# Attention heads in pairs, the recurrent part's preparation moved ahead of the second attention, and small matmuls in idle stretches of a two-block transformer kernel

## What is computed

```
state = state * wt + sa * bt + vt * kt        # per head, 64 x 64, sa = state @ at
y = state @ rt
```

## Time and profile before

| | |
|---|---|
| runs | 2500.05, 2499.9, 2498.51 us, median 2499.9 |
| profiled execution | 2497.89 us, its span 2496.2 us |
| mean granted clock of PE | 0.941 |
| bytes read | 614.26 MB, 246 GB/s over the span |
| instructions | 35200 |

### The profile page before, as it was taken

The page is one execution under the profiler, slowest core; times in us unless marked ns, Lnnn a source line. Parts: engine busy times, 40 slices in busy tenths (PEclk is TensorE's granted clock), DMA queues, the critical chain, the costliest instruction groups (busy, mean ns, idle before and its releaser), DMA issues.

```text
span 2496.2 us, 35200 instructions
## 1 busy us (share of the span) xinstructions
PE 2269.5 (91%) x14178; PEld 1936.6 (78%) x14178; DVE 1726.6 (69%) x1706; ACT 1370.3 (55%) x1273; POOL 93.4 (4%) x154
## 2 busy tenths in 40 slices
PE   4997999799799999999999999987995886999986
PEld 2966899795788888888888888876975785888876
DVE  1764444635578888888888888855446447899954
ACT  2225333435367777777777777753443234677743
POOL 8300000001000000000000000000000000000000
PEclk7998999899799999999999999998987887999988
DMA  8665765348259999999999999977620131899930
GB/s 261 198 204 175 238 233 187 113 152 281 91 203 368 379 372 370 371 371 371 370 373 370 370 371 367 375 226 101 192 64 2 36 135 46 306 371 374 371 137 18
DMA packets 339250, 618.72 MB, mean 248 GB/s; under 512 B 24609, under 2 KB 165154, under 8 KB 339087
## 3 DMA queue, kind: packets, MB, share of 16 engines
q1 hardware_dynamic: 339086, 616.43, 70.7%
HBM read 614.26 MB, written 1.05 MB: 246 GB/s over the span
## 4 chain that ended last, share of the span: by engine, by line
PE 88%; DVE 6%; ACT 2%; issue 2%; SPq 1%; DMA 1%; DVEq 0%; POOL 0%; ACTq 0%; POOLq 0%
PE bank L1146 11%; PE bank L1147 11%; PE bank L1148 11%; PE bank L2045 6%; PE bank L2046 6%; PE bank L2047 6%; PE bank L1178 5%; PE bank L1180 5%; PE bank L1176 5%; PE bank L2082 2%; PE bank L2155 2%; PE bank L2116 1%; PE bank L1119 1%; PE bank L2111 1%; PE bank L1156 1%
## 5 line engine op out<-in xcount | busy, mean ns | idle before, releaser
L1351 DVE TENSOR_TENSOR ring_lo<-ring_raw,ring_hi 128x2048 fp32r<-128x2048 f32 x432 | 988.1, 2291 | 140.1 <-ACT ring_hi L1261 139.5
L1261 ACT ACTIVATE ring_hi<-ring_raw 128x2048 fp32r<-128x2048 f32 x432 | 827.8, 1920 | 289.2 <-PE bank L1148 181.4
L1146 PE MATMUL bank<-ring_hi,xg_hi 128*128 128x512 f32 x1152 | 458.0, 398 | 2.1 <-DVE xg_lo L1451 2.1
L1147 PE MATMUL bank<-ring_hi,xg_lo 128*128 128x512 f32 x1152 | 451.0, 391 | 0.0
L1148 PE MATMUL bank<-ring_lo,xg_hi 128*128 128x512 f32 x1152 | 450.7, 391 | 0.0
L2045 PE MATMUL bank<-Hh,ring_hi 128*128 128x256 f32 x1048 | 307.2, 293 | 56.3 <-DVE ring_lo L454 23.0
L454 DVE TENSOR_TENSOR ring_lo<-ring_raw,ring_hi 128x2048 fp32r<-128x2048 f32 (+1 forms) x96 | 218.0, 2282 | 188.3 <-ACT ring_hi L436 165.1
L2046 PE MATMUL bank<-Hl,ring_hi 128*128 128x256 f32 x1048 | 303.9, 290 | 0.0
L2047 PE MATMUL bank<-Hh,ring_lo 128*128 128x256 f32 x1048 | 303.6, 290 | 0.0
L2045 PEld LDWEIGHTS bank<-Hh,ring_hi 128*128 128x128 f32 x1048 | 209.0, 199 | 59.6 <-issue 48.5
L1146 PEld LDWEIGHTS bank<-ring_hi,xg_hi 128*128 128x128 f32 x1152 | 217.5, 189 | 48.0 <-ACT xg_hi L1304 2.9
(11 more groups left out here) (475 smaller groups left out, 2764.3 us busy)
## 6 DMA issues: line engine op xcount, KB each, us to landing
ring_raw<-in_moe_w SPq DMA_DIRECT2D x672, 512.0 KB, 5.2
ring_raw<-in_ada_w SPq DMA_DIRECT2D x96, 512.0 KB, 5.9
ring_raw<-in_ffn_w SPq DMA_DIRECT2D x66, 512.0 KB, 4.9
ring_raw<-in_exp_gate SPq DMA_DIRECT2D x64, 512.0 KB, 4.8
ring_raw<-in_exp_up SPq DMA_DIRECT2D x64, 512.0 KB, 4.7
ring_raw<-in_exp_down SPq DMA_DIRECT2D x64, 512.0 KB, 4.7
ring_raw<-in_w_in SPq DMA_DIRECT2D x42, 512.0 KB, 4.9
ring_raw<-in_conv_in_w SPq DMA_DIRECT2D x16, 512.0 KB, 8.4
```

The costliest lines, as they stand in the source:

```text
L1146: mm(o, xg_hi[:, g, kk, :], wh(k), start=(kk == 0), stop=False)
L1147: mm(o, xg_lo[:, g, kk, :], wh(k), start=False, stop=False)
L1261: run(ring_hi[:, s, :], ring_raw[:, n % RAW, :], ACT.Copy).then_inc(T.sem("hi_done"), 1)
L1351: tt(ring_lo[:, s, :], ring_raw[:, n % RAW, :], ring_hi[:, s, :].bitcast(F32), ALU.subtract).then_inc(T.sem("lo_done"), 1)
```

## The change

1. **Preparation.** Its steps are cut into functions and put between the column units of block 2, on PE, ACT and DVE. Its tiles get other homes, for the old ones are in use then. The head mask `m_d64` is built on POOL after "shifted", not after a2. ACT waits for "decayed" ahead of a2's softmax.
2. **Heads in pairs.** `attention` goes over pairs: the scores of two heads are issued alternately into two banks, their values alternately into two halves of one bank. The rings `pr` and `small` have four slots, not three, and ACT evicts outputs later.
3. **Convolution.** Block 5 keeps 17 of its 31 taps on PE; DVE adds the other 14 after PE's sum is evicted. PE has 79 taps, five between two adaptive units.
4. **Splits.** At the feed-forward's end the last split ahead of ln1 is the one two units ahead, not three.
5. **Small matmuls.** `keep_busy(n)` issues n fp32 matmuls of 128 columns, whose results nobody reads, into the bank that is next to be taken: six between mean and variance of all nine layer norms, and 16 to 28 at other places, 302 in all.
6. **Tokens of the second expert stage** are written contiguously, and PE reads its stationary blocks with a step of four elements.

The diff, cut to its core (the moved functions `lora_pe`, `gate_lora_pe`, `head_sums_pe`, `shift_act`, `lora_act`, `gate_lora_act`, `norm_act`, `decay_act`, `keys_dve`, `decay_dve`, `norm2_dve`, `mixed_key_dve`, `normal_dve`, `bonus_dve` and `decayed_dve` hold the same operations as before, in part on other tiles, and are left out; `normal_dve` does them in two halves):

```diff
+            pairs = heads // 2
+            half = lambda h: (h // 2, slice(64 * (h % 2), 64 * (h % 2) + 64))
+
+            def scores(j):
+                b = [take(pe, f"{name} s {2 * j + n}") for n in range(2)]
+                pe.eng.wait_ge(*T.at(f"{name} qT {j // 2}"))
+                pe.eng.wait_ge(*T.at(f"{name} kT {j // 2}"))
+                for n in range(2):
+                    k, r = half(2 * j + n)
+                    mm(b[n][:, 0:P], Q[r, k, 0:P], K[r, k, 0:P], start=True, stop=True)
+                for n in range(2):
+                    k, r = half(2 * j + n)
+                    mm(b[n][:, P:3 * P], Q[r, k, P:S], K[r, k, :], start=True, stop=True)\
+                        .then_inc(pe.tick(f"mm {name} s {2 * j + n}"), 1)
+
+            def turned(j):
+                for h in (2 * j, 2 * j + 1):
                     b = take(pe, f"{name} pT {h}", "B")
                     pe.eng.wait_ge(*T.at(f"{name} p {h}"))
                     for c in range(3):
-                        last = nc.tensor.transpose(b[:, c * P:(c + 1) * P], pr[:, h % 3, c * P:(c + 1) * P],
+                        last = nc.tensor.transpose(b[:, c * P:(c + 1) * P], pr[:, h % 4, c * P:(c + 1) * P],
                                                    ident[:, :])
                     last.then_inc(pe.tick(f"mm {name} pT {h}"), 1)
-                if i >= 3:
-                    h = i - 3
-                    k, r = h // 2, slice(64 * (h % 2), 64 * (h % 2) + 64)
-                    if h % 2 == 0:
-                        bank_o[k] = take(pe, f"{name} o {k}", "C")
-                    b = bank_o[k]
-                    pe.eng.wait_ge(*T.at(f"{name} pT {h}"))
-                    pe.eng.wait_ge(*T.at(f"{name} v"))
-                    hs = slice(64 * h, 64 * h + 64)
-
-                    mm(b[r, 0:S], V[:, 0, hs], prT[:, h % 3, 0:2 * P], start=True, stop=False,
+
+            def values(j):
+                b = take(pe, f"{name} o {j}", "C")
+                pe.eng.wait_ge(*T.at(f"{name} v"))
+                for n in range(2):
+                    pe.eng.wait_ge(*T.at(f"{name} pT {2 * j + n}"))
+                for n in range(2):
+                    h = 2 * j + n
+                    mm(b[half(h)[1], 0:S], V[:, 0, 64 * h:64 * h + 64], prT[:, h % 3, 0:2 * P], start=True, stop=False,
                        skip_group_check=True)
-                    mm(b[r, P:S], V[:, 1, hs], prT[:, h % 3, 2 * P:3 * P], start=False, stop=True,
-                               skip_group_check=True).then_inc(pe.tick(f"mm {name} o {h}"), 1)
-
-
-
-
+                for n in range(2):
+                    h = 2 * j + n
+                    mm(b[half(h)[1], P:S], V[:, 1, 64 * h:64 * h + 64], prT[:, h % 3, 2 * P:3 * P], start=False,
+                       stop=True, skip_group_check=True).then_inc(pe.tick(f"mm {name} o {h}"), 1)
+
+            for j in range(pairs + 2):
+                if j < pairs:
+                    scores(j)
+                if between:
+                    between(2 * j)
+                    between(2 * j + 1)
+                if 1 <= j <= pairs:
+                    turned(j - 1)
+                if j >= 2:
+                    values(j - 2)
...
-            h, q = 512 * (j // 2), slice(64 * (j % 2), 64 * (j % 2) + 64)
-            return [t[:, :, h:h + 512].rearrange("p a (k q) -> p a q k", k=4)[:, :, q, :] for t in both] + \
-                [b.rearrange("p a (q k) -> p a q k", k=4)]
+                return t[:, kk * P:(kk + 1) * P]
+            h = 512 * (kk // 4)
+            return t[:, h:h + 512].rearrange("p (q k) -> p k q", k=4)[:, kk % 4, :]
...
+        SHARED, ON_PE = KT - PE_BLOCKS, 17
+        pe_taps = [(k, i) for k in pe_blocks for i in range(ON_PE if k == SHARED else TAPS)]
+        last_tap = lambda k: ON_PE - 1 if k == SHARED else TAPS - 1
...
-            for _ in range(6):
+            for _ in range(5):
...
+            def keep_busy(n, group="A"):
+
+                b = GROUPS[group][T.rot.get(group, 0) % len(GROUPS[group])]
+                if T.occupant.get(b):
+                    pe.eng.wait_ge(*T.at("ev " + T.occupant[b]))
+                for _ in range(n):
+                    mm(bank[b][:, 0:P], ident[:, :], means[:, :], start=True, stop=True)
+
+            pe.keep_busy = keep_busy
+
+            def ln_stats(name, z, before=0, behind=0):
+
+                pe.eng.wait_ge(*T.at("means"))
+                if before:
+                    keep_busy(before)
                 b = take(pe, "ln " + name)
-                pe.eng.wait_ge(*T.at("means"))
                 for k in range(KT):
                     pe.eng.wait_ge(*T.at(f"z {name} {k}"))
                     last = mm(b[:, 0:S], means[:, :], z[:, k, :], start=(k == 0), stop=(k == KT - 1))
                 last.then_inc(pe.tick(f"mm mean {name}"), 1)
+                keep_busy(6)
                 b = take(pe, "lv " + name)
                 for k in range(KT):
                     pe.eng.wait_ge(*T.at(f"square {name} {k // 2}"))
                     last = mm(b[:, 0:S], means[:, :], tC[:, k, :], start=(k == 0), stop=(k == KT - 1))
                 last.then_inc(pe.tick(f"mm var {name}"), 1)
+                if behind:
+                    keep_busy(behind)
...
+            keep_busy(28, "C")
...
+            keep_busy(20, "C")
...
-            ln_stats("ln1", tA)
+            ln_stats("ln1", tA, 18, 20)
...
-            ln_stats("ln2", tA)
+            ln_stats("ln2", tA, 0, 16)
             pe.stage = "m1"
             moe_pe(pe, m1, tD)
             rest_pe(pe, m1, tD)
-            ln_stats("ln3", tA)
+            ln_stats("ln3", tA, 26, 16)
...
+            ln_stats("ln4", tA, 0, 20)
             for j in range(8):
                 columns(("rw", j), f"rw {j}", Hh, Hl, None if j else "b2")
             for j in range(2):
                 rows_of(("v2", j), f"v2 {j}", Hh, Hl)
-            for key in ("q2", "k2"):
-                for j in range(2):
-                    columns((key, j), f"{key} {j}", Hh, Hl)
-            for j in range(4):
+            lora_pe(pe)
+            columns(("q2", 0), "q2 0", Hh, Hl)
+            gate_lora_pe(pe)
+            columns(("q2", 1), "q2 1", Hh, Hl)
+            head_sums_pe(pe, "ss", norms, "k squared")
+            for j in range(2):
+                columns(("k2", j), f"k2 {j}", Hh, Hl)
+            columns(("ga", 0), "ga 0", Hh, Hl)
+            head_sums_pe(pe, "rk", wide, "r k")
+            for j in range(1, 4):
...
+            keep_busy(18)
...
+            ln_stats("ln5", tA, 0, 16)
...
+            ln_stats("ln6", tA, 18, 0)
             pe.stage = "ple"
             pe.eng.wait_ge(*T.at("p landed"))
             transposes("pT", [(2 * k + a, p_in[:, a, k * P:(k + 1) * P]) for k in range(2) for a in range(TT)])
+            keep_busy(16)
...
+            ln_stats("ln7", tA, 0, 16)
...
-            split_hi(act, at_unit[("ffn2", NP - 1)] + 3)
+            split_hi(act, at_unit[("ffn2", NP - 1)] + 2)
...
+                if j == 0:
+                    shift_act(act)
             T.mark("a2 v", *act.last)
+            lora_act(act)
...
+                    if key == "q2" and j == 0:
+                        gate_lora_act(act)
+                    if key == "k2" and j == 0:
+                        norm_act(act)
...
+                if j == 1:
+                    decay_act(act)
             T.mark("gate a", *act.last)
+            act.eng.wait_ge(*T.at("decayed"))
...
+            dve.eng.wait_ge(*T.at(f"ev dw {SHARED}"))
+            for i in range(ON_PE, TAPS):
+                stt(tA[:, SHARED, :], uT[:, SHARED, i:i + S], col("conv_dw_w", SHARED, i), tA[:, SHARED, :],
+                    ALU.mult, ALU.add).then_inc(dve.tick(f"z conv {SHARED}"), 1)
+                dve.eng.wait_ge(*dve.own())
...
-            for key, n in (("v2", 2), ("q2", 2), ("k2", 2), ("ga", 4)):
-                for j in range(n):
-                    split_lo(dve, at_unit[(key, j)] + 2)
+            split_lo(dve, at_unit[("v2", 0)] + 2)
+            split_lo(dve, at_unit[("v2", 1)] + 2)
+            split_lo(dve, at_unit[("q2", 0)] + 2)
+            keys_dve(dve)
+            decay_dve(dve)
+            split_lo(dve, at_unit[("q2", 1)] + 2)
+            norm2_dve(dve)
+            split_lo(dve, at_unit[("k2", 0)] + 2)
+            mixed_key_dve(dve)
+            split_lo(dve, at_unit[("k2", 1)] + 2)
+            normal_dve(dve, 0)
+            split_lo(dve, at_unit[("ga", 0)] + 2)
+            normal_dve(dve, 1)
+            split_lo(dve, at_unit[("ga", 1)] + 2)
+            bonus_dve(dve)
+            split_lo(dve, at_unit[("ga", 2)] + 2)
+            decayed_dve(dve)
+            split_lo(dve, at_unit[("ga", 3)] + 2)
```

More of the change, by code:

```diff
@@ L503, in rwkv_pe, with head_sums_pe @@
+        def head_sums_pe(pe, name, tile, ready):
+            pe.eng.wait_ge(*T.at("head mask"))
+            pe.eng.wait_ge(*T.at(ready))
+            for j in range(2):
+                b = take(pe, f"{name} {j}", "D")
+                for i in range(2):
```

(2 more changed lines are left out.)

257 lines of the change are left out of this document (139 added, 118 removed).

## The result

The changed kernel takes 2439.57 us (median of 4 runs, 2436.97 to 2442.91) against 2499.2 before (4 runs, 2498.03 to 2500.05): a ratio of 0.9762, with a 95% interval of 0.9746 to 0.9779. It is faster by 59.6 us, and inside the forecast's range of 2412 to 2460, 8.6 us above its 2431. The profiled execution took 2440.48, its span is 2438.8.

What follows compares the result with a forecast made beforehand. PE, busy 91% of the span, bounds the kernel, so only shortening its work or gaps pays. From 2497.9 us, −27.9 − 12 − 6.5 − 1.7 − 17.5 − 1.3 = −66.9 gives 2431; range 2412 to 2460.

Steps and rivals of the forecast that it cites:

- the rival of starved units: Column units: low splits come late behind DVE's preparation pieces; preparation gives −15, not −27.9, time 2444; chance 0.14.
- 20.3 was forecast for it: Second attention: DVE at 1.83 a head, 14.6 for eight, plus 5.7 for first softmax's latency and last head's turn and values.
- the +1.3 for the late key unit: Split moved behind ln1: the split is then late for the third key unit, costing 1.3 us.
- The rule of the step: Norms: a mean costs 6.59 us at half clock, the same work 3.71 at full; fillers that keep the clock save the difference.
- the list of places: Clock gains: ln3, ln4, ln6 up to 2.9 each; conv norm 4.3, conv start 1.3, w_out 2.0, others 5; stated sum −18.5.
- as the rival had it: Second expert stage's gather: strided stationary reads cost +6.4 to +13 us, time 2441; chance 0.05.
- Part 5: Small matmuls in idle time keep PE's clock: −18.5, fillers in nine norms +1.0, −17.5 us; bounds −22 to +10.
- part 1: Recurrent part's preparation moves ahead of the second attention, between column units: 81.2 to 53.3 us, −27.9; bounds −35 to −12.
- part 4: One split moved behind ln1: −3.0 on the path into the mean, +1.3 for a late split, −1.7 us; bounds −3 to +1.
- The rival of a clock that doesn't answer: Fillers run inside idle time but don't keep the clock: small matmuls give 0 to +1 us, time 2449; chance 0.14.
- that of pairs that don't overlap: Attentions: alternate products wait for one another, losing the pairs' gain, +12 and +8 us, time 2451; chance 0.09.
- the slower one: Fillers on PE's in-order queue overrun the idle time: 2494 us at 0.47 a filler, 2600 at 0.82; chance 0.03.

Runs made afterwards that it cites:

- e7: Changed kernel with another order in the second attention alone, scores of pairs ahead of values: 2438.12 us (4 runs).
- e8: Order of e7, plus 30 small matmuls behind the second attention's first scores and a dummy exponential on ACT for the early table load: 2435.34 us, ratio 0.9735.
- e11: Changed kernel with pairs kept, but each head's two matmuls issued together instead of by turns: 2434.7 us (one run).
- e6: Changed kernel with the second expert stage's tokens written strided and read contiguously, as before the change: 2443.52 us (one run).
- e2: Changed kernel with attention heads one at a time and ACT's eviction order as before, rings of four slots kept: 2461.28 us (one run).
- e4: Changed kernel with all 31 taps of block 5 on PE and six taps between adaptive units, as before: 2447.44 us (one run).
- e5: Changed kernel with the feed-forward's last split again three units ahead instead of two: 2450.35 us (one run).
- e1: Changed kernel without any small matmuls: 2446.88 us (4 runs), ratio to before 0.9786.
- e9: Kernel of e8 with the second attention's values directly behind the next scores, and 20 instead of 6 small matmuls in norms conv and ln0: 2433.47 us, ratio 0.9728.
- e12: Kernel of e8 with 20 instead of 6 small matmuls between mean and variance of norms conv and ln0: 2429.72 us (5 runs), ratio 0.972.
- e10: Changed kernel with twice the small matmuls at every place (604): 2462.48 us (4 runs), ratio 0.9848.

## Why the prediction was right, and where it missed

1. **The preparation: -27.9 forecast, -25.1 measured.** The units ahead grew by 9.8 (forecast 10.6), and PE had no gap in them (busy 110.84 of 111 us), so the rival of starved units is refuted: DVE's pieces, up to 6.1 us at once (1762.5 to 1768.6), fitted, with the splits two units ahead, which was the forecast's reason and wasn't tried by itself. From the end of the units, where the first score starts, to the first bias it took 5.2 (forecast 5.9; the 1.4 that I gave for before is DVE's idle time ahead of its first bias, and the like stretch was 1.05), the units behind 14.8 (forecast 16.5). The term that was mis-sized is the attention itself: 20.3 was forecast for it, by DVE at 1.83 a head, and 25.9 came (1812.18 to 1838.10). I had named PE's half clock as a thing of the kernel before, and then reckoned as if DVE alone set the pace. Of the 5.6 that it took longer, e7 puts at most 1.0 down to the order of PE's work, and e8 1.3 to the table load, for which the sum has no term, and some 2.8 to the clock; with these gone it takes 20.8. With the same code, the stretch from ln4's variance to the recurrent part takes from 167.3 (e11) to 170.3 us (e6), 194.6 before, so the part gives 24.3 to 27.2: the attention's miss is clear, that of the whole part hardly.
2. **Pairs: -12 forecast, -12.2 measured,** and e2 gives 13.2 by undoing them. Row halves and column halves both overlap, as the earlier trace rows had it.
3. **Convolution: -6.5 forecast, 7.1 with the conv start's clock, and 6.7 by e4.** Right.
4. **The split: -1.7 forecast, -3.0 at ln1's mean and -4.5 at ln2's by e5, in one run.** The sign was right. The step "-3.0" for the mean fits (3.0 against the changed kernel, 1.4 to 3.4 against all like it); the +1.3 for the late key unit is there as a wait (1.24), but the stretch is no shorter without it. With one run, -1.7 isn't refuted.
5. **Small matmuls: -17.5 forecast, -7.3 measured by e1.** This is the largest miss, and the stated sum is wrong by itself: the places listed (8.7 for ln3, ln4 and ln6, then 4.3, 1.3, 2.0 and 5) add up to 21.3, not 18.5, so the term should have read -20.3, and the forecast 2428. The rule of the step, 6.6 less 3.7 at each norm, held at ln3, ln4 and ln6 (2.8, 2.8 and 3.0). The failed step is the list of places: the norm conv with its output units, for which I had 4.3, gave 0.3 up to ln0's mean, since six matmuls cover 1.5 us of a gap of 5.2, and in the 3.9 us left the clock falls; ln1 needed none; the stage of `w_out` gave 0.8 for 2.0 against the kernel before (3.8 by e1, in part not the small matmuls'). The conv start gave 1.8 by e1, for 1.3. e9 and e12 show that the norm's place can be had, with 20.
6. **Tokens: -1.3 forecast, 1.6 by the eviction.** The strided loads take 100 ns longer each, as the rival had it, but cost no 6.4 us: at most 0.8. The Trainium skill ("Advanced Engine Details and Errata", SBUF Cachelines) says that a different 16-byte line at each access is penalised; the trace agrees for the load (on the mean 315 against 209 ns), and the measured time decides that it is hidden beside the products for the most part.

Trace against trace the gain is 57.4 us where 66.9 was forecast. Part 5 had 10.2 too much and part 1 2.8, part 4, taken at 4 between its two figures, 2.3 too little; the three others together 1.1 too little. That leaves less than a microsecond, but several of these sizes are only good to 1 or 2 us, and by its trace e1 gives 9.0 for part 5, so the fit is in part luck. So is it that the forecast lies only 8.6 off: added up rightly it would have been some 11 off. The rival of a clock that doesn't answer is refuted by e1 and e8, that of pairs that don't overlap by e2, and the slower one by the result; e10 shows its mechanism at work at twice the number, 22.9 us, still 37 us under the kernel before.

## What to carry to other kernels

When a stage is short of work on one engine and the stage ahead of it leaves two others half idle, move the work; but then look at what the bound engine does in the few microseconds around the seam, since an idle stretch of 8 us there put most of the attention at half clock, and a table load stood behind the wait. Taking both away made the attention 4.1 us shorter, some 2.8 of it by the clock. Idle time of PE ahead of a chain of small products is worth filling nearly up to its end and not beyond: too short a filling gave nothing at the norm conv and was worse than none at ln0, and each matmul past the end is a loss of up to 0.23 us. Products of two heads that use different halves of the array overlapped when they stood together in PE's program, by turns or not. And before a difference of a few microseconds in one stage is put down to an edit, look at how much that stage differs between traces that have the same code in it.

## What was not expected of the hardware

**Stages that no edit touches differ by some microseconds.** From the start of ln2's variance to that of ln3's mean, over the first expert stage, nine of the traces have 1034.4 to 1036.3 us and four (e2, e5, e6, e9) 1038.4 to 1038.5, with the same code there but for the small matmuls (e10, with twice as many, is left out). The 3 us have a place: behind the stage, DVE loads a value and branches on it (L1651, `If`), and then issues nothing for 1.69 us in one execution and 4.73 in another. The chain of the changed kernel, and that of e9:

```profile
1658.57 2.59 DVEq L1651
1661.15 1.69 issue
```

```profile
1654.71 2.58 DVEq L1661
1657.30 4.73 issue
...
1663.06 6.12 PE bank L2224 x16
```

With 4.73, the 26 small matmuls ahead of ln3 end 6 us before the mean in place of 1.4, the clock falls, and the mean takes 6.1 us in place of 3.7: the delay of 3 us costs 5.4. The same four traces have 4.71 to 4.73 there and that mean at 6.1; in the nine others it is 1.43 to 1.70. It may be why the changed kernel's runs spread by 6 us where those of the kernel before, whose mean is at half clock anyway, spread by 2; that was argued, not shown. Why the branch takes 1.7 or 4.7 was not tried.

**Neighbours need not take turns.** In e11 the first head's two products and then the second head's two ran in the same 0.8 us as by turns, and the second head's first product ran ahead of the first head's second. How far apart two such products may stand and still overlap was not tried, but in e2, with other work between the heads, they didn't.
